# Moving the product of the last 4096 modulation columns from VectorE to four column groups of TensorE

## The reference, cut to what matters

```python
def modulate(h, shift, scale):
    return h * (1 + scale) + shift

def adaln_params(cond, w_mod, b_mod):
    m = jax.nn.silu(cond) @ w_mod + b_mod
    return [t[..., None, :] for t in jnp.split(m, N_MOD, axis=-1)]

sh_m, sc_m, gt_m, sh_f, sc_f, gt_f = adaln_params(c, w_mod[i], b_mod[i])
h_lat = modulate(rmsnorm(x, g_norm_mix[i]), sh_m, sc_m)
...
x = x + gt_m * mix_lat
h = modulate(rmsnorm(x, g_norm_ffn[i]), sh_f, sc_f)
x = x + gt_f * moe_ffn(h, w_router[i], b_router[i], w_gate_up[i], b_gate_up[i],
                       w_down[i], b_down[i])
```

## Time and profile before

| | |
|---|---|
| median of 3 runs | 1665.02 us (1663.82 to 1665.15) |
| the profiled execution | 1667.85 us |
| its span | 1666.0 us |
| granted TensorE clock over the span | 0.924 of full speed |
| PE busy | 1387.7 us, 83% |
| PEld busy | 565.5 us, 34% |
| DVE busy | 469.2 us, 28% |
| ACT busy | 320.3 us, 19% |
| POOL busy | 226.9 us, 14% |

### The profile page before, as it was taken

The page is one execution under the profiler, slowest core; times in us unless marked ns, Lnnn a source line. Parts: engine busy times, 40 slices in busy tenths (PEclk is TensorE's granted clock), DMA queues, the critical chain, the costliest instruction groups (busy, mean ns, idle before and its releaser), DMA issues.

```text
span 1666.0 us, 18855 instructions
## 1 busy us (share of the span) xinstructions
PE 1387.7 (83%) x6257; PEld 565.5 (34%) x6258; DVE 469.2 (28%) x1065; ACT 320.3 (19%) x539; POOL 226.9 (14%) x156
## 2 busy tenths in 40 slices
PE   4798997698999998787778779899978787998892
PEld 2585476332333332222222223233322222332230
DVE  2998776411211121111111112121211111211114
ACT  3334621111111111111111111111111111111112
POOL 1731253000001000000000000000000000110011
PEclk9899988799999999999899989999988899999996
DMA  9747134469665679999999995966999998179884
GB/s 378 238 154 261 44 124 156 162 235 386 228 225 205 207 242 384 389 386 389 384 384 386 388 382 207 380 240 248 364 385 381 385 377 296 20 254 382 311 303 143
DMA packets 200002, 474.56 MB, mean 285 GB/s; under 512 B 11250, under 2 KB 11762, under 8 KB 198961
## 3 DMA queue, kind: packets, MB, share of 16 engines
q1 hardware_dynamic: 189154, 455.20, 73.5%
q0 software_dynamic: 10832, 19.16, 5.5%
HBM read 463.05 MB, written 18.35 MB: 289 GB/s over the span
## 4 chain that ended last, share of the span: by engine, by line
PE 42%; DMA 37%; DVE 10%; SPq 7%; issue 2%; ACT 1%; POOL 0%; POOLq 0%; DVEq 0%
DMA ring<-in_w_gate_up 34%; PE ps L1359 27%; PE ps L1368 8%; SPq L407 7%; DVE bc L808 3%; DMA wm<-in_w_mod 2%; PE ps L1354 1%; PE ps L1378 1%; PE ps L1242 1%; PE ps L1343 1%; DVE cv L824 1%; PE ps L1234 1%; DVE Um L887 1%; DVE xl L1108 1%; DMA wm_b<-in_w_mod 0%
## 5 line engine op out<-in xcount | busy, mean ns | idle before, releaser
L1359 PE MATMUL ps<-ring,xT 128*64 128x512 f32 x2880 | 702.0, 639 | 178.3 <-DMA ring<-in_w_gate_up 178.3
L1359 PEld LDWEIGHTS ps<-ring,xT 128*64 128x64 f32 x2880 | 223.2, 147 | 587.3 <-issue 586.8
L1368 PE MATMUL ps<-ring,aT 128*64 128x512 f32 x1440 | 338.8, 602 | 0.0
L1073 DVE TENSOR_SCALAR gb<-ps 128x256 f32<-128x256 f32 x90 | 38.2, 425 | 1043.7 <-PE ps L1359 1043.7
L514 POOL DMA_INDIRECT y_rows<-osb,idx_c x46 | 72.3, 1572 | 722.1 <-ACT osb L697 704.4
L701 ACT ACTIVATE sg<-gb 128x256 f32<-128x256 f32 x90 | 37.5, 416 | 573.2 <-DVE gb L1073 573.2
L1368 PEld LDWEIGHTS ps<-ring,aT 128*64 128x64 f32 x1440 | 91.4, 136 | 149.9 <-issue 146.8
L501 POOL DMA_INDIRECT xg<-h_rows,idx_n x46 | 45.2, 982 | 515.9 <-DVE idx_n L984 515.9
L694 ACT ACTIVATE aT<-ps 128x256 f32<-128x256 f32 x90 | 34.5, 383 | 357.9 <-PE ps L1378 357.9
L712 ACT ACT_TABLE_LOAD x45 | 57.7, 1283 | 0.8
L697 ACT ACTIVATE osb<-ps,gate_c 128x512 f32<-128x512 f32 x46 | 31.6, 687 | 135.5 <-PE ps L1368 134.9
(11 more groups left out here) (255 smaller groups left out, 1099.4 us busy)
## 6 DMA issues: line engine op xcount, KB each, us to landing
ring<-in_w_gate_up SPq DMA_DIRECT2D x128, 2048.0 KB, 19.7
ring<-in_w_down SPq DMA_DIRECT2D x64, 2048.0 KB, 20.1
wm<-in_w_mod SPq DMA_DIRECT2D x4, 2048.0 KB, 21.9
wm_a<-in_w_mod SPq DMA_DIRECT2D x4, 2048.0 KB, 9.0
wm_b<-in_w_mod SPq DMA_DIRECT2D x4, 2048.0 KB, 8.6
win<-in_w_in SPq DMA_DIRECT2D x3, 2048.0 KB, 20.5
x_in<-in_x SPq DMA_DIRECT2D x1, 2048.0 KB, 10.9
wo_f<-in_w_out SPq DMA_DIRECT2D x1, 2048.0 KB, 7.3
```

The source lines that it names most:

```text
L1359: last = MMUL(ps[M * j:M * (j + 1), h, :].rearrange("m (g n) -> m g n", g=2), xT[:, k, :], ring[:, 2 * h:2 * h + 2, k, j * GW:(j + 1) * GW ...
L1368: last = MMUL(ps[M * y:M * (y + 1), 2, :], aT[:, h, i, M * j:M * (j + 1)], chunk_dst(4 + h)[:, k, y * YW:(y + 1) * YW], start=False, stop= ...
```

## The change

The last 4096 columns are computed like the first 2048. The weights come as eight loads of [128, 2, 2048]: two blocks of 128 rows, 2048 columns (8 KB in a row where there were 2 KB). `z_rows_of(i)`, called "block i" below, makes from each load eight products, 2 row blocks by 4 column groups, with one stationary column; blocks 0 to 3 add up in bank 4 and blocks 4 to 7 in bank 5, in partitions 0, 32, 64 and 96. VectorE copies the eight pieces of a row to row 0 of `bc` (`z_row`, four copies each). `b_mod` is loaded to row 1 of `bc`, and `z_sum` multiplies two rows of ones with the two rows of `bc`. The zeroing of `bc` goes. Since banks 4 and 5 are taken, the four GELU inputs use banks 6 and 7 in turn, so L(6) and L(7) wait for a GELU, and L(8) and L(9) wait for the two `z_row` copies. The buffers `wm_a` and `wm_b` are free again when PE has read them (`z_used`), not when VectorE has (`z_ready`).

```diff
-        wm_rest = [at("wm_a", [P, KD, CH], ZD), at("wm_b", [P, KD, CH], ZD + 16 * KB)]
+        wm_rest = [at("wm_a", [P, 2, 2 * D], ZD), at("wm_b", [P, 2, 2 * D], ZD + 16 * KB)]
...
-            sp.wait_ge(S["bc_zero"], 1)
-            load(bc[0:1, :, :].rearrange("p a d -> p (a d)"), b_mod[2 * D:6 * D].partition_broadcast(1), "ld_bc")
+            sp.wait_ge(S["xs_ready"], TC + TL)
+            load(bc[1:2, :, :].rearrange("p a d -> p (a d)"), b_mod[2 * D:6 * D].partition_broadcast(1), "ld_bc")
...
-                    sp.wait_ge(S["z_ready"], i - 1)
-                load(wm_rest[i % 2][:, :, :], wm_v[:, :, (4 + i) * CH:(5 + i) * CH], f"ld_zm{i % 2}")
+                    sp.wait_ge(S["z_used"], i - 1)
+                m, k = i // 4 + 1, i % 4 * 2
+                load(wm_rest[i % 2][:, :, :], wm_v[:, k:k + 2, m * 2 * D:(m + 1) * 2 * D], f"ld_zm{i % 2}")
...
-                sp.wait_ge(S["z_ready"], 7 + i)
+                sp.wait_ge(S["z_used"], 7 + i)
...
-            pool.wait_ge(S["xs_ready"], TC + TL)
-            nc.gpsimd.memset(bc[:, :, :], 0.0).then_inc(S["bc_zero"], 1)
...
-                A(gelu[:, t, :], ps[:, 4 + t, :], ACT.Gelu_apprx_tanh).then_inc(S["gelu_done"], 1)
+                A(gelu[:, t, :], ps[:, 6 + t % 2, :], ACT.Gelu_apprx_tanh).then_inc(S["gelu_done"], 1)
...
-            def z_chunk(i):
-
-                dve.wait_ge(S[f"ld_zm{i % 2}"], 16 * (i // 2 + 1))
-                if i == 0:
-                    dve.wait_ge(S["ld_bc"], 16)
-                W, Z = wm_rest[i % 2], bc[:, i // 2, (i % 2) * CH:(i % 2 + 1) * CH]
-                for k in range(KD):
-                    ins = V.scalar_tensor_tensor(Z, W[:, k, :], csil[:, k, 0:1], Z, ALU.mult, ALU.add)
-                    if k < KD - 1:
-                        link(ins)
-                ins.then_inc(S["z_ready"], 1)
-
-            z_chunk(0)
-            z_chunk(1)
+            def z_row(m):
+
+                dve.wait_ge(S["z_used"], 4 * m + 4)
+                if m == 0:
+                    dve.wait_ge(S["xs_ready"], TC + TL)
+                for q in range(4):
+                    n = 4 * m + q
+                    V.tensor_copy(bc[0:1, n // 2, (n % 2) * CH:(n % 2 + 1) * CH], ps[32 * q:32 * q + 1, 4 + m, :]).then_inc(S["z_ready"], 1)
...
-                if t:
-                    z_chunk(t + 1)
+                if t == 1:
+                    z_row(0)
...
-            for i in range(RT + 1, 8):
-                z_chunk(i)
+            z_row(1)
...
+            def z_rows_of(i):
+                pe.wait_ge(S[f"ld_zm{i % 2}"], 16 * (i // 2 + 1))
+                if i == 4:
+                    pe.wait_ge(S["film_ready"], 1)
+                for k in range(2):
+                    for q in range(4):
+                        last = MMUL(ps[32 * q:32 * q + 1, 4 + i // 4, :], csil[:, i % 4 * 2 + k, 0:1],
+                                    wm_rest[i % 2][:, k, q * CH:(q + 1) * CH], start=(i % 4 == 0 and k == 0), stop=(i % 4 == 3 and k == 1))
+                last.then_inc(S["z_used"], 1)
+
+            z_rows_of(0)
             latents(0, 2, True)
+            z_rows_of(1)
             latents(1, 3)
+            z_rows_of(2)
             pe.wait_ge(S["hc_lo"], 1)
             for t in range(RT):
                 if t >= 2:
                     pe.wait_ge(S["xr_copied"], t - 1)
                     latents(t, 2 + t % 2)
                 context(t, t % 2).then_inc(S["xr_done"], 1)
+                z_rows_of(3 + t)
             pe.wait_ge(S["mm_copied"], 1)
             for t in range(RT):
-                latents(4 + t, 4 + t).then_inc(S["gr_done"], 1)
+                if t >= 2:
+                    pe.wait_ge(S["gelu_done"], t - 1)
+                latents(4 + t, 6 + t % 2).then_inc(S["gr_done"], 1)
+                if t == 0:
+                    z_rows_of(7)
             for g in range(GT):
-                pe.wait_ge(S["gelu_done"], g + 1)
+                if g < 2:
+                    pe.wait_ge(S["z_ready"], 4 * g + 4)
+                else:
+                    pe.wait_ge(S["gelu_done"], g + 1)
                 latents(8 + g, 4 + g).then_inc(S["f_done"], 1)
...
-                pe.wait_ge(S["z_ready"], i + 1)
-                MMUL(ps[:, 2 + i % 2, :], ones, bc[:, i // 2, (i % 2) * CH:(i % 2 + 1) * CH], start=True, stop=True).then_inc(S["z_done"], 1)
+                if i == 0:
+                    pe.wait_ge(S["z_ready"], 8)
+                    pe.wait_ge(S["ld_bc"], 16)
+                MMUL(ps[:, 2 + i % 2, :], ones[0:2, :], bc[0:2, i // 2, (i % 2) * CH:(i % 2 + 1) * CH], start=True, stop=True).then_inc(S["z_done"], 1)
```

More of the change, by code:

```diff
@@ L279, in build @@
             ld_zm0 ld_zm1 ld_dft ld_bc ld_gnf ld_wo0 ld_wo1 ld_xl ld_wr ld_bias ld_gfin dve_step act_step
-            pool_step csil_ready mod_done mod_copied mod_turned bc_zero t_done t_by_act t_by_dve mean_in
+            pool_step csil_ready mod_done mod_copied mod_turned z_used t_done t_by_act t_by_dve mean_in
             root_in mean_ffn film_ready edges_zero wbd_zero bf_ready ssq_in xs_ready hl_by_act hl_by_dve
```

## The result

| | before | changed |
|---|---|---|
| median of the runs | 1664.43 us (1663.82 to 1665.15, 4 runs) | 1676.36 us (1674.65 to 1679.26, 4 runs) |
| ratio, 95% interval | | 1.0073 [1.0056, 1.0091] |
| a second set of 4 runs (a_again, below) | 1665.52 us | 1678.58 us, 1.0082 [1.0062, 1.0103] |
| the profiled execution, its span | 1667.85, 1666.0 us | 1679.26, 1677.4 us |

Every ratio in this document is taken against runs of the kernel before that were made beside the runs in question; their medians were 1666.88 us for e1 to e4, 1665.52 us for a_again, h1 and the runs with 32 and 64 rows, and 1665.08 us for those with 96 and 127 rows.

The account below looks back on a forecast made before the run. PE was taken to bound the stretch ahead of T, VectorE the place behind it. 5.0 + 6.1 = 11.1 us lost less 8.1 gained gave +3.0 on 1665.0, 1668.0 us; range 1663.5 to 1672.5.

Parts of the forecast that it names:

- Part 1: Behind `gates(0)`: VectorE is free for the Fourier copies, so drive(0) starts 8.5 us after T, not 16.6; 8.1 us gained.
- T: The end of `gates(0)`, 147.2 us before the change; forecast to move back by 11.1 us, to about 158.3.
- Rival D: Behind T: a copy waits longer for PE, VectorE isn't freed, the 8.1 us are lost; +11, 1676 us; chance 0.02.
- Part 2: Price of one block on PE: 1.71 us of MATMULs plus 0.17 on each side for switching tiling, 2.05 us.
- Part 3: Blocks 0 to 2 cost nothing: they fill PE's idle time, and C(0) then runs at full clock.
- Part 4: Block 3's load lands at 74.5 us, PE waits 1.5 us, and L(2) starts 5.0 us later.
- the second working, from the bytes: Block 3's load time worked out from bytes and transfer rates: 57.2 + 18.5 - 1.3 = 74.4 us.
- Rival B: The wait for block 3 lets PE's clock fall: +4.6 to +7.6, middle +6, 1671.0 us; chance 0.23.
- Part 5: Blocks 5, 6 and 7 stand in PE's full stretch and cost 3 x 2.05 = 6.1 us.
- Part 6: Small things, among them the `z_row` copies, GELU waits, `z_sum` with as many columns and the zeroing of `bc`: all nothing.
- The sum: Whole kernel: 11.1 us lost ahead of T less 8.1 gained behind it, +3.0 us, 1668.0 us on the median.
- rival A: The load of block 3 is in time: T moves by 9.6, so +1.5, 1666.5 us; chance 0.20.

Follow-up runs that it names:

- a_again: The changed kernel unaltered, run once more: 1678.58 us, 1.0082.
- e1: The changed kernel with 128 rows in `z_sum` again, `bc` zeroed by GpSimd: 1671.18 us, 1.0029.
- e4: The changed kernel with 128 rows in `z_sum` and the loads of `win0` and the router's weights behind block 5's: 1664.7 us, 0.9992.
- h1: e4 with only columns 2048 to 4095 (blocks 0 to 3) on PE, columns 4096 to 6143 back on VectorE: 1657.63 us, 0.9958.
- e3: The changed kernel with the loads of `win0` and the router's weights moved behind block 5's load: 1672.45 us, 1.0032.
- e6_127rows: e4 with 127 rows in `z_sum` in place of 128: ratio 1.0014.

## Why the prediction was wrong

- **Part 1, what goes behind T: right.** Drive(0) starts 8.1 us behind T, forecast 8.5, before 16.6, so the gain is 8.5 us where 8.1 were forecast. No gap, four copies of `fT` early, 1.38 us of waiting for the last copy of `Y`. Rival D did not come.
- **Part 2, 2.05 us for a block: right.** 2.05 from e3, 1.99 from h1 against e4. The MATMULs alone show 1.90 us, forecast "about 1.9". The rest of the 2.05 is the time until the next product can begin, as in the earlier trace rows. With the Trainium skill's rule that a change of mode must drain (TensorEngine Tiling (Array Packing), Key Properties) the runs agree; they don't separate the two sides of the block.
- **Part 3, blocks 0 to 2 hidden, C(0) at full clock: right.** Block 2 starts at 67.77 (forecast 67.9).
- **Part 4, block 3's load: a term mis-sized.** The load landed at 75.7 and 75.3 us in the two profiles, forecast 74.5, bounds no wait at all (73.0) to 77.5. SP issued block 2's load 1.2 us sooner than I had it (53.03, not 54.2), and that brought nothing: the span to the landing grew from 20.35 to 22.7 us. I had counted from an issue. In e3, with `win0` and the router's weights no longer ahead of it, the load was there before PE at 72.65 us; so what stands ahead in the queue decides. Why the second working, from the bytes (74.4), was also about a microsecond short, no run shows. PE waited 2.6 to 3.0 us and not 1.5.
- **Rival B, the clock behind that wait: in one profile of three.** 3.34 us for block 3 in the first, 1.90 in the second and in e1, which has the same loads. Of T's extra delay (13.9 against 11.1) the wait is 1.5 and the slow block 1.4 us. "It decides from a wait somewhere between 1.5 and 2.5 us" is refuted: 2.57 and 2.65 us kept the clock here, 3.01 didn't, and with the 2.47 us of the earlier trace rows that lost it no single length fits.
- **Part 5, blocks 5 to 7 in full: right**, by h1.
- **Part 6 is the step that failed.** "`z_sum` has as many columns as before", all nothing. The columns were right and the rows were overlooked. The products on both sides of the wait for ACT went from full to two rows, PE's clock stayed at half for 20 us, and in that stretch PE is the engine that everything waits for. Price: +8.0 us in `z_sum` and the square sums, +5.2 in the leg of the first profile, 7.3 by e1's ratio and 6.7 by e3 and e4. With this step alone undone (e1) the ratio is 1.0029, 1669.8 us on the median before, inside the range. Had I laid a product with its wait of 3.07 us beside the earlier trace rows, whose waits of 2.47 and 3.21 us both ended in half clock, I would have seen that the stage might stand on the edge, and would have kept the rows or booked a rival for it.
- **The sum.** +3.0 forecast, +2.8 for T (Part 4 and B in that profile), -0.4 for Part 1 and +5.2 for Part 6 make +10.6 us, the measured difference at residual(0); the medians give +11.9. Ahead of drive(0) the first profile is rival B's case (+5.4, its middle was +6), and the second (a_again) is +3.4, near the forecast. With both repaired (e4) drive(0) starts 0.5 us later than before and the ratio is 0.9992, which is near rival A's case of a load in time.

## What to carry to other kernels

Ask of every product that changes shape what it does to the clock of the products behind it, not only how many columns it streams: fewer rows saved nothing here and cost about 7 us, and the zero rows that had seemed waste were worth them. Move work to a bounded engine only as far as it finds idle time there: three of the eight blocks were free and the gain behind T was had with four, so half the change won 0.4% where the whole lost 0.7%. And when a load must be there sooner, look at what stands ahead of it in the queue: here an issue 1.2 us earlier behind the same transfers brought nothing.

## What the runs showed of the hardware

- Products of 512 columns with 2, 32 or 64 rows, begun behind an idle 2.9 us, took 10.2 to 10.6 us for twelve in all six profiles that had them, a granted 0.50 to 0.52, and the full-row work behind them began at 0.50 too: in the changed kernel it rose only 10 us later. With 96 rows the twelve took 8.88 us, with 127 7.21 us, with 128 5.61 to 7.21 us, behind nearly the same wait (3.1 us).
- Not every wait of one length ends alike: 3.07 and 3.08 us ahead of `z_sum` kept the clock in two profiles (before, e4) and lost it for a while in three (e1, e6_127rows, h1). It was worth 1.5 us in the twelve, and its rule stays open.
- A wait isn't needed. In all six profiles whose first square sums (products of 128 rows and one moving column) ran at or near full clock, the clock fell to 0.50 at their end, for 3 to 7 us of PE busy without a break: a mean of 0.66 over 5 us before, 0.59 in e4.
- Products with one stationary column on column tiles, but all 128 rows, kept the clock at full behind waits of 2.57 and 2.65 us. So a small number of stationary columns did not lower it here. The Trainium skill says of the clock that the throttled state is the default and activity releases it (TensorE: Matmul & The Clock Gate, The HAM clock gate). The falls behind PE's waits agree with that; the rows show besides that a PE which is busy all the time can stay at half clock, as from 212 to 232 us in the changed kernel.
